# Inverses of 16x16 diagonal blocks on VectorE in a chunked RWKV-7 recurrence, and three small steps moved to ScalarE in the stage ahead of it

## The reference, cut to what matters

```python
w_log = -jax.nn.softplus(-(p["w0"] + jnp.tanh(wd) @ p["w_up"]).astype(f32)) - 0.5
decay = jnp.exp(-jnp.exp(w_log))
a = jax.nn.sigmoid((p["a0"] + ad @ p["a_up"]).astype(f32))
...
def step(S, inp):
    r_t, w_t, k_t, v_t, kk_t, a_t = inp
    sa = jnp.einsum('bhvk,bhk->bhv', S, -kk_t)
    S = (S * w_t[:, :, None, :] + sa[..., None] * (kk_t * a_t)[:, :, None, :]
         + v_t[..., None] * k_t[:, :, None, :])
    return S, jnp.einsum('bhvk,bhk->bhv', S, r_t)
```

## Time and profile before

| | us |
| --- | --- |
| median of 3 runs (1785.7 to 1789.13) | 1786.02 |
| the profiled execution | 1785.42 |
| its span | 1783.7 |
| from the recurrence's first matmul, 535.20, to the end of its last, 849.68 | 314.48 |
| of that, up to `scores_k` of chunk 1 (561.64) | 26.44 |
| up to `scores_k` of chunk 8 (769.88) | 208.24 |
| the rest, with the two stream chunks | 79.80 |

### The profile page before, as it was taken

How to read it: one execution, slowest core, us unless ns; L and a number is a source line. 1 busy time by engine, 2 the same in 40 slices (tenths; PEclk the granted TensorE clock), 3 DMA queues, 4 the chain that set the end, 5 groups by cost and what they waited for, 6 DMA issues and landing times.

```text
span 1783.7 us, 40832 instructions
## 1 busy us (share of the span) xinstructions
PE 1628.9 (91%) x17188; PEld 1513.3 (85%) x17188; DVE 892.6 (50%) x1196; ACT 459.2 (26%) x670; POOL 569.2 (32%) x353
## 2 busy tenths in 40 slices
PE   6899999998659999998897999977999999999995
PEld 6899999997229999997477989944999999999995
DVE  4489999432795656565652664042632112211247
ACT  4222222234441111111212234232233212211221
POOL 2555551136460000000144411201644534443541
PEclk9999999999659999999779999998999999999997
DMA  4212253224000000101413144245212222222222
GB/s 154 71 59 75 78 74 88 90 99 150 26 0 4 4 4 4 41 20 42 153 35 142 59 138 157 98 160 209 81 60 82 71 79 74 71 80 73 71 82 82
DMA packets 54749, 140.03 MB, mean 79 GB/s; under 512 B 22208, under 2 KB 24768, under 8 KB 52592
## 3 DMA queue, kind: packets, MB, share of 16 engines
q1 hardware_dynamic: 53360, 133.15, 23.5%
q0 software_dynamic: 1280, 5.24, 0.7%
HBM read 125.38 MB, written 12.99 MB: 78 GB/s over the span
## 4 chain that ended last, share of the span: by engine, by line
PE 55%; issue 19%; DVE 10%; POOL 10%; ACT 3%; DMA 1%; POOLq 0%; DVEq 0%; SPq 0%; ACTq 0%; PEldq 0%
PE ps L375 33%; PE ps L487 15%; POOL wlo L353 7%; POOL hdl L1695 2%; PE ps L1753 1%; DVE x L800 1%; PE ps L1874 1%; DMA kc<-in_kc 1%; DVE p_L L1396 1%; DVE ar L1453 1%; DVE acc L1300 1%; PE ps L1801 1%; PE ps L1773 1%; DVE ar L1416 1%; PE ps L1883 0%
## 5 line engine op out<-in xcount | busy, mean ns | idle before, releaser
L353 POOL TENSOR_TENSOR wlo<-raw,whi 128x1024 fp32r<-128x1024 f32 x150 | 382.7, 2551 | 555.1 <-ACT whi L342 554.7
L342 ACT ACTIVATE whi<-raw 128x1024 fp32r<-128x1024 f32 x158 | 166.7, 1055 | 282.7 <-PE ps L375 275.5
L375 PE MATMUL ps<-xnl,whi 128*128 128x320 f32 x672 | 154.5, 311 | 7.5 <-POOL xnl L444 6.1
L375 PE MATMUL ps<-fnl,whi 128*128 128x320 f32 x704 | 160.7, 309 | 0.0
L375 PE MATMUL ps<-fnh,wlo 128*128 128x320 f32 x704 | 160.5, 309 | 0.0
L375 PE MATMUL ps<-fnh,whi 128*128 128x320 f32 x704 | 160.3, 309 | 0.0
L375 PE MATMUL ps<-xnh,wlo 128*128 128x320 f32 x672 | 153.7, 310 | 0.0
L375 PE MATMUL ps<-xnh,whi 128*128 128x320 f32 x672 | 153.6, 310 | 0.0
L375 PEld LDWEIGHTS ps<-xnl,whi 128*128 128x128 f32 x672 | 113.1, 189 | 8.3 <-issue 6.4
L1300 DVE SCALAR_TENSOR_TENSOR acc<-up,vec,acc 128x512 f32<-128x512 f32 x240 | 118.3, 560 | 0.0
L375 PEld LDWEIGHTS ps<-fnl,whi 128*128 128x128 f32 x704 | 117.8, 188 | 0.3
(11 more groups left out here) (323 smaller groups left out, 3533.8 us busy)
## 6 DMA issues: line engine op xcount, KB each, us to landing
raw<-in_slots SPq DMA_DIRECT2D x174, 512.0 KB, 3.5
kc<-in_kc SPq DMA_DIRECT2D x4, 2048.0 KB, 8.7
vc<-in_vc SPq DMA_DIRECT2D x8, 1024.0 KB, 8.8
xin<-in_x SPq DMA_DIRECT2D x4, 640.0 KB, 8.0
tmp_g<-tmp POOLq DMA_DIRECT2D x8, 320.0 KB, 2.5
tmp_m<-pr POOLq DMA_DIRECT2D x8, 320.0 KB, 3.8
m1t<-tmp_m SPq DMA_DIRECT2D x1, 2560.0 KB, 11.7
t2t<-tmp_g SPq DMA_DIRECT2D x1, 2560.0 KB, 17.7
```

What stands on the lines that cost most here:

```text
L342: nc.scalar.activation(whi[s][:].rearrange("p a b -> p (a b)"), raw[s][:], ACT.Copy).then_inc(S["w_hi"], 1)
L353: on.tensor_tensor(wlo[s][:].rearrange("p a b -> p (a b)"), raw[s][:], whi[s][:].rearrange("p a b -> p (a b)").bitcast(F32), ALU.subtract) ...
L375: last = nc.tensor.matmul(cut(ps[s], h, n), a[:, k, :], b[:, k, h * w:(h + 1) * w], start=(k == 0 and q == 0), stop=(k == k_tiles - 1 and ...
```

## The change

**In the recurrence** the first four levels, those up to 16x16 blocks, leave PE. DVE masks the scores so that only the 16x16 diagonal blocks are left (`ndt`) and sums the four column blocks over each other into `nd`, 16 columns wide. SP carries these by 8 transfers per chunk into `blk` (`rec_blocks`, L504 after), where a partition holds one block of one head; two chunks with 64 blocks each fill the 128 partitions. There DVE inverts all 128 at once: `inverse_level` for sizes 2, 4 and 8 multiplies small matrices as products written out along the free dimension (`product`) and their sums (`summed`). 16 more transfers (L511 after) carry the inverses and their transposes back into `xd`, and ScalarE spreads them by four copies, each with a scale per partition that is 1 or 0, into `x2` (`inverse_in`). PE keeps two levels, here called `level_t(k, 0)` with `level_4` and `level_t(k, 1)` with `level_5`, and for the stream chunks none. Since a pair of chunks is inverted together, `scores_b` runs ahead: both of a pair are made in the even chunk before, and `scb` gets four buffers. `turn_v` uses another PSUM bank.

**In the preparing stage** DVE's subtraction for `p_m` goes: ScalarE takes the exponential of `p_L` shifted by one token, in two instructions, and DVE writes the ones at the starts of the chunks beforehand by four memsets. The copies into `wcum` go from POOL to ScalarE. PE waits for `rn` only at the product that reads it. A few semaphores are joined and counted anew.

```diff
+        def rec_blocks(sp, m):
+            for e in range(2):
+                sp.wait_ge(S["nd_ready"], nth(2 * m + e, 1))
...
+                for t in range(8):
+                    p0 = 64 * e + 8 * t
+                    sp.dma_start(blk[p0:p0 + 8, :, :], nd[e][:, t, :]).then_inc(S["block_in"], 16)
+            sp.wait_ge(S["inv_step"], 2 + INV_STEPS * (m + 1))
+            for e in range(2):
+                if m:
+                    sp.wait_ge(S["x_made"], 4 * (2 * m + e - 1))
+                for t in range(8):
...
+                    sp.dma_start(xd[e][:, t, :, :].rearrange("p n c -> p (n c)"), inv[p0:p0 + 8, :, :, :].rearrange("p r n c -> p r (n c)"))\
+                        .then_inc(S["xd_in"], 16)
...
+            scores_b(0)
+            scores_b(1)
             for k in range(NCH + 1):
                 j = k - 1
-                scores_b(k)
                 scores_k(k)
                 if k:
                     right_side(j)
-                level_0(k)
+                if k < NCH:
+                    level_t(k, 0)
                 turn_bk(k)
                 if k:
                     solve(j, 3)
-                level_t(k, 1)
+                if k < NCH:
+                    level_4(k)
                 if k:
                     new_state(j)
-                level_x(k, 1)
+                if k < NCH:
+                    level_t(k, 1)
+                if k < NCH and k % 2 == 0:
+                    scores_b(k + 2)
                 turn_v(k)
-                level_t(k, 2)
+                if k < NCH:
+                    level_5(k)
                 if k:
                     outputs(j, 3)
-                level_x(k, 2)
-                for L in range(3, levels(k)):
-                    level_t(k, L)
-                    level_x(k, L)
+                if k < NCH and k % 2 == 0:
+                    scores_b(k + 3)
...
+            def inverse_in(c):
+                w("xd_in", 256 * (c // 2 + 1))
+                if c >= 2:
+                    w("u_psum", nth(c - 2, 1))
+                for q in range(4):
+                    nc.scalar.activation(x2[c % 2][:, :, :, 16 * q:16 * q + 16], xd[c % 2][:].rearrange("p t n c -> p n t c"), ACT.Copy,
+                                         scale=cst[:, CCOL["stream"] + q:CCOL["stream"] + q + 1]).then_inc(S["x_made"], 1)
...
+            for m in range(CHUNKS // 2):
+                rec_blocks(sp, m)
             sp.wait_ge(S["bk_made"], 2 * NCH)
...
+                for (dst, first), (src, _) in zip(by_run(p_m[s]), by_run(p_L[s])):
+                    last = nc.scalar.activation(dst[:, :, 1:first], src[:, :, 0:first - 1], ACT.Exp, scale=-DECAY / 2)
+                last.then_inc(S["e_ready"], 1)
...
-                nc.scalar.activation(p_m[s][:], p_m[s][:], ACT.Exp, scale=-DECAY / 2).then_inc(S["e_ready"], 1)
...
+                nc.scalar.activation(wcum[:, j, 0:NCH], p_e1[s][:, C - 1:SEQ:C], ACT.Copy)
+                nc.scalar.activation(wcum[:, j, NCH:NCH + NS], p_e1[s][:, SEQ + TS - 1:NT:TS], ACT.Copy).then_inc(S["e_ready"], 1)
...
-            pe.wait_ge(S["rn_ready"], 2)
...
+                else:
+                    pe.wait_ge(S["rn_ready"], 2)
...
-                done(nc.vector.tensor_tensor(p_m[s][:], p_L[s][:], p_l[s][:], ALU.subtract))
```

More of the change, by code:

```diff
@@ L459, in program @@
         CHUNKS = NCH + 2
-        def levels(c):
-            return LEVELS if c < NCH else STREAM_LEVELS
+        INV_STEPS = 16
         def rows_of(c):
@@ L471, in nth, with lv @@
             return 2 * c + g + 1
[L473 to L479, removed]
+        def lv(c, l, g):
+            return 4 * c + 2 * l + g + 1
         def four(a):
@@ new lines, in product @@
+            def product(m, n, size, left, right):
+                dve.wait_ge(S["inv_step"], 2 + INV_STEPS * m + n)
+                nb = 8 // size
+                out = prod[:, 0:nb * size ** 3].rearrange("p (b i c j) -> p b i c j", b=nb, i=size, c=size)
+                for b in range(nb):
+                    last = tt(out[:, b, :, :, :], left[:, b, :, :].rearrange("p i (c j) -> p i c j", c=1).to_broadcast([P, size, size, size]),
+                              right[:, b, :, :].rearrange("p j (i c) -> p i c j", i=1).to_broadcast([P, size, size, size]), ALU.mult)
+                last.then_inc(S["inv_step"], 1)
+                return out
@@ new lines, in summed, with inverse_level @@
+            def summed(m, n, out, terms):
+                dve.wait_ge(S["inv_step"], 2 + INV_STEPS * m + n)
+                nc.vector.tensor_reduce(out=out, in_=terms, op=ALU.add, axis=AX.X).then_inc(S["inv_step"], 1)
+            def inverse_level(m, size):
+                n = {2: 1, 4: 5, 8: 9}[size]
+                upper = diagonal_blocks(low, 32, 0, size)
+                corner = diagonal_blocks(low[:, size:, size:], 32, 0, size)
+                side = diagonal_blocks(low, 32, size, size)
+                given = diagonal_blocks(blk, 16, size, size)
+                part = half_prod[:, 0:8 * size].rearrange("p (b i c) -> p b i c", b=8 // size, i=size)
+                summed(m, n + 1, part, product(m, n, size, upper, given))
+                summed(m, n + 3, side, product(m, n + 2, size, part, corner))
@@ L787, in level_0 @@
-                    tt(x2[k % 2][:, :, gs[g], :], x2[k % 2][:, :, gs[g], :], one, ALU.add).then_inc(S["x_new"], 1)
-            def level_t(k, L):
-                for g in range(2):
-                    w("t_ready", lv(k, L, g))
-                    tt(td[:, gs[g], :], four(bank(g, 0)[:, 0:256]), step(L), ALU.mult).then_inc(S["t_new"], 1)
-            def level_x(k, L):
-                n = slice(1 if L == levels(k) - 1 else 0, 2)
-                for g in range(2):
-                    w("x_ready", lt(k, L, g))
-                    w("x_new", lv(k, L - 1, g))
-                    x = x2[k % 2][:, n, gs[g], :]
-                    tt(x, bank(g, 0)[:, :].rearrange("p (n t c) -> p n t c", n=2, t=4)[:, n], x, ALU.add).then_inc(S["x_new"], 1)
+                    w("x_ready", lv(k, 0, g))
```

294 lines of the change are left out of this document (188 added, 106 removed).

## The result

The changed kernel takes 1769.43 us (median of 4 runs, 1763.05 to 1770.24) against 1785.86 of the kernel before in the same comparison: 0.9901 of it, with a 95% interval of 0.9885 to 0.9916. It is faster, by 16.4 us where 47 were forecast; 1769 lies in the range of 1720 to 1782, but not in the forecast's own, 1719 to 1766. The profiled execution took 1763.05 us, with a span of 1761.4.

The account below looks back on a forecast made before the run. PE was taken to bound the recurrence. Recurrence −35.9, earlier wait −4.8 and tiles −6.6 make −47.3 from 1785.42, so 1738.1, forecast as a median of 1739 us (chance 0.64); range 1720 to 1782, its own 1719 to 1766.

Parts of the forecast that it names:

- What bounds the kernel, and what the removed records are worth: Recurrence, chunks 1 to 7: PE bounds it, working 202.43 of 208.24 us; a pair's remaining records take 36.8 us.
- The new wait and its place: First remaining level of even chunks: PE waits 15.4 us for the inverses, 6.4 covered, so it stands 9.0 us.
- The term of 7.1: SP's 16 issues carrying inverses back, inside PE's wait: 15 × 0.47 = 7.1 us to the last issue.
- The first rival: SP issues the block transfers at 0.81 us, not 0.47: +38.4, 1777 us in all; chance 0.13.
- DVE's part of the wait: From PE's last odd-chunk level: addition 0.42, level over 512 2.76, two copies 0.58, a further 0.9: 4.7 us.
- ScalarE's copies: Four copies of the inverses at the end of PE's wait: 1.3 us.
- The clock: After a stand of PE the clock is at 0.50 for 5.3 us; taken as 2.5 us lost a pair.
- The second rival: The clock stays at 0.50 for the whole even chunk after a stand: +31.5, 1770 us; chance 0.08.
- The way in costs nothing: Transfers of blocks for DVE's inverse: DVE waits 5.6 us for the second eight, but PE loses nothing.
- The third rival: SP's queue takes no issue until earlier transfers leave: slower from 0.88 us each, 1803 us at 1.0; chance 0.12.
- The sums: Recurrence: chunk 0 +20.5, chunks 1 to 7 −46.6, chunk 8 onwards −9.8; together −35.9 us.
- The preparing stage: Ahead of the recurrence: −4.8 us since the first low-rank product skips the reciprocal's wait, −6.6 over eight tiles.

Follow-up runs that it names:

- the other two: The changed kernel itself, without any edit, run and profiled twice more to look at the spread: 1769.50 us (0.9896) and 1771.11 us (0.9912).

## Why the prediction was right or wrong

- **What bounds the kernel, and what the removed records are worth:** right. Without the carrying a pair takes 38.05 us, 36.8 of it as counted.
- **The new wait and its place:** right; its size was wrong, and this is the step that failed. "Short issues on SP's queue begin 0.47 apart": these begin 0.65 to 0.70 apart. The row was of other transfers. The term of 7.1 measures 9.7 to 10.5, twice in the front and once in each pair and at the end. The first rival (0.81) had the right mechanism and too large a price. By its own slope, 90 issues that nothing hides at 0.20 more, the miss is 18 us. The nearer price stood in the trace of the kernel before: 0.81 is the mean of the 16 loads at 746.33, of which a few are long, up to 1.68; their median length is 0.63.
- **DVE's part of the wait:** 5.5 for 4.7. Not the waits between dependent steps, for which I had 0.9 and which come to some 0.2. The two multiplications over 512 elements with repeated operands took 1.03 and 1.05, for which I had 0.69 from a plain reduction; the reductions took 0.69. And from PE's end at 647.3 to the end of DVE's additions, at 648.6, it is 1.4 where 0.42 was counted, because DVE still had the inverse's level before, until 648.0. **ScalarE's copies:** 1.7 for 1.3; its copies of the rearranged `xd` take longer than the plain ones of the earlier trace rows. **The landing:** about 2.0 for 2.3.
- **The clock:** right, 2 to 2.5 us a pair as shown by filling PE. The second rival (low for a whole chunk) is out: it is back behind some 5 us, and that its 1770 is so near the measured time is chance.
- **The way in costs nothing:** nearly. DVE waits there 3.6 to 5.3 us in each odd chunk, but PE stands at their second level only in chunks 1 and 7, for 0.5 and 1.4. **The third rival** (a queue that stops issuing) is out: transfers overlap, since ScalarE starts 2.0 us after the last of 16 issues, and the issues are 0.67 apart. The rule of the Trainium skill that the prediction weighed, in "DMA: Bandwidth & Descriptors", section "Rules for kernel authors", that under 64 KB one pays mostly overhead, holds here: of 0.65 to 0.70 us some 0.5 are the same whatever a transfer carries. That transfers would come in series is not in that rule; it was the prediction's own reading of it.
- **The sums:** front +25.5 (forecast +20.5), chunks 1 to 7 −32.2 (−46.6), end −7.4 (−9.8): −14.1 for −35.9 in the first profile, −13.3 and −11.6 in the other two. Of the 14.4 missed in the chunks, 3 × 3.9 are the longer stands.
- **The preparing stage:** −5.9 for −11.4. The moved wait gave 3.3 of 4.8, since the first tile's exponentials wait again; the tiles gave some 2.6 of 6.6. Two tiles lose 0.82 + 1.98 = 2.8 us of subtraction; 1.3 of it comes back in `p_b`, which now runs beside GpSimd's product, and 0.6 to 1.6 in waits for ScalarE, which the prediction took to be off the tiles' path. In the changed kernel itself the tiles fall otherwise, the last product being slow in six of the eight and before in four, but the stage takes as long as with its part alone: from the first scan to the clearing of the state 527.43 − 451.77 = 75.7 us, and 529.54 − 453.91 = 75.6 there.
- So the 30 us are about 22 of recurrence, 18 of them by the length of the issues, and 5.5 of preparing stage; what is left is within the spread above, which the forecast had left out.

## What to carry to other kernels

Price a transfer by its issue on one queue, and look for a row of the same kind of transfer (from SBUF to SBUF, cut in as many rows); many small ones in a chain cost their number times the issue, so spread them over queues whose engines are idle, and put the waiting engine's other work ahead of the wait. When an instruction leaves an engine, look at whom its old partner slowed: a saving on DVE was more than half lost because what is left runs beside GpSimd and waits for ScalarE.

## What the runs showed of the hardware that I had not expected

- The issue of a transfer from SBUF to SBUF on SP's queue is 0.60 us long for 16 KB in 128 rows, 0.61 for 8 KB in 128 rows and 0.54 for 8 KB in 64 rows (medians). From start to start it is 0.65 to 0.70, 0.66 to 0.73 and 0.59. With SP and ScalarE issuing at once it is 0.68 to 0.84 on either queue, and on GpSimd's queue 0.59 (a group's length divided by its 8).
- A DVE multiplication over 512 elements with repeated operands takes 1.03 to 1.05 us, a reduction over as many 0.69.
- DVE's product of 640 elements takes 2.16 and its scan 2.82 while GpSimd works on its products, 0.82 and 1.48 otherwise.
- Behind three stands of 2.07 us in one run the granted clock was twice 1.00 and once 0.53, and behind one of 1.91 (PE filled, chunk 4) it was 1.00; behind each one of 3.1 us or more that was looked at it fell to 0.50 for some microseconds.
